# A hybrid decoder layer with 32 experts on one core: expert biases copied into the accumulation banks ahead of each block of tokens, in place of one-hot matmuls

## The reference, cut to what matters

```python
def expert_block(args):
    xe, e = args
    gu = xe @ w_gu[e] + b_gu[e]                 # 1024 -> 2048, gate and up interleaved
    gate = jnp.minimum(gu[..., 0::2], SWIGLU_LIMIT)
    up = jnp.clip(gu[..., 1::2], -SWIGLU_LIMIT, SWIGLU_LIMIT)
    act = (up + 1.0) * (gate * jax.nn.sigmoid(gate * SWIGLU_ALPHA))
    return act @ w_dn[e] + b_dn[e]              # 1024 -> 1024
```

## Time and profile before

| | us |
|---|---|
| median of 3 runs | 1615.03 |
| lowest and highest | 1613.72, 1615.38 |
| profiled execution | 1609.29 |
| its span | 1607.5 |
| PE, DVE, ACT, Pool busy in it | 1479.8, 1293.3, 1020.8, 236.1 |
| granted TensorE clock, mean | 0.956 of full |

### The profile page before, as it was taken

One profiled execution on the slowest core, in us unless ns is written; L12 is line 12 of the kernel. 1 busy time (PEld: TensorE's weight loads), 2 busy tenths in 40 slices (PEclk: granted clock), 3 DMA queues, 4 the chain that ended last, 5 costly groups with the idle time before them and its releaser, 6 DMA issues.

```text
span 1607.5 us, 20866 instructions
## 1 busy us (share of the span) xinstructions
PE 1479.8 (92%) x7011; PEld 1227.5 (76%) x7011; DVE 1293.3 (80%) x1228; ACT 1020.8 (64%) x902; POOL 236.1 (15%) x148
## 2 busy tenths in 40 slices
PE   5999889755899999999999999999999999999983
PEld 5777667644788888888888888888888888888872
DVE  5227753474899999999999999999999999999991
ACT  5335433313677777777777777777777777777771
POOL 0000000000011122211111222111112211111120
PEclk9999999657999999999999999999999999999996
DMA  9311030604899999999999999999999999999974
GB/s 349 105 54 53 27 131 13 223 24 180 304 347 377 385 370 372 382 388 381 388 381 379 375 372 381 385 388 381 387 376 378 375 374 384 385 386 386 377 263 131
DMA packets 97674, 486.12 MB, mean 302 GB/s; under 512 B 8217, under 2 KB 8242, under 8 KB 63794
## 3 DMA queue, kind: packets, MB, share of 16 engines
q1 hardware_dynamic: 87250, 448.05, 71.3%
q0 software_dynamic: 10400, 37.75, 9.0%
HBM read 461.65 MB, written 24.12 MB: 302 GB/s over the span
## 4 chain that ended last, share of the span: by engine, by line
PE 87%; issue 5%; DVE 5%; DMA 2%; ACT 1%; SPq 0%; DVEq 0%; POOLq 0%; POOL 0%; ACTq 0%
PE gu_bank L1031 17%; PE gu_bank L1032 17%; PE gu_bank L1033 17%; PE turn_bank L1031 8%; PE turn_bank L1032 8%; PE turn_bank L1033 8%; PE gu_bank L1226 2%; PE bank L1233 2%; PE bank L1240 2%; PE bank L1031 1%; PE bank L1165 1%; PE bank L1033 1%; PE bank L1032 1%; DVE w_lo L697 1%; PE turn_bank L1148 1%
## 5 line engine op out<-in xcount | busy, mean ns | idle before, releaser
L697 DVE TENSOR_TENSOR w_lo<-raw,w_hi 128x2048 fp32r<-128x2048 f32 x412 | 934.9, 2289 | 129.1 <-ACT w_hi L493 125.0
L493 ACT ACTIVATE w_hi<-raw 128x2048 fp32r<-128x2048 f32 x412 | 789.5, 1920 | 238.9 <-PE gu_bank L1033 184.1
L1031 PE MATMUL gu_bank<-w_hi,turned 128*128 128x512 f32 (+1 forms) x1104 | 432.3, 392 | 7.0 <-DVE turned L950 7.0
L1032 PE MATMUL gu_bank<-w_lo,turned 128*128 128x512 f32 (+1 forms) x1104 | 429.3, 389 | 0.0
L1033 PE MATMUL gu_bank<-w_hi,turned 128*128 128x512 f32 (+1 forms) x1104 | 429.1, 389 | 0.0
L1031 PEld LDWEIGHTS gu_bank<-w_hi,turned 128*128 128x128 f32 x1104 | 208.2, 189 | 49.2 <-issue 5.8
L1033 PEld LDWEIGHTS gu_bank<-w_hi,turned 128*128 128x128 f32 x1104 | 208.1, 188 | 42.8
L1032 PEld LDWEIGHTS gu_bank<-w_lo,turned 128*128 128x128 f32 x1104 | 208.3, 189 | 41.5
L1031 PE MATMUL turn_bank<-w_hi,turned 128*128 128x512 f32 (+1 forms) x544 | 211.5, 389 | 2.0 <-DVE turned L955 2.0
L1032 PE MATMUL turn_bank<-w_lo,turned 128*128 128x512 f32 (+1 forms) x544 | 211.0, 388 | 0.0
L1033 PE MATMUL turn_bank<-w_hi,turned 128*128 128x512 f32 (+1 forms) x544 | 210.3, 387 | 0.0
(11 more groups left out here) (206 smaller groups left out, 1354.5 us busy)
## 6 DMA issues: line engine op xcount, KB each, us to landing
raw<-in_w_gate_up_dram SPq DMA_DIRECT2D x264, 1024.0 KB, 8.8
raw<-in_w_down_dram SPq DMA_DIRECT2D x132, 1024.0 KB, 10.9
raw<-in_w_in_dram SPq DMA_DIRECT2D x10, 1024.0 KB, 8.3
raw<-in_w_out_dram SPq DMA_DIRECT2D x4, 1024.0 KB, 5.2
raw<-in_w_mem_kv_dram SPq DMA_DIRECT2D x2, 1024.0 KB, 8.7
arena<-in_x_dram SPq DMA_DIRECT2D x1, 2048.0 KB, 14.4
arena<-in_position_tables_dram SPq DMA_DIRECT2D x1, 2048.0 KB, 19.5
arena<-in_x_dram SPq DMA_DIRECT2D x2, 1024.0 KB, 5.5
```

Source lines behind the costliest of these rows:

```text
L493: a.activation(w_hi[:, slot, :], raw_ap, ACT.Copy).then_inc(hi_ready, 1)
L697: v.tensor_tensor(w_lo[:, slot, :], raw_ap, w_hi[:, slot, :].bitcast(F32), ALU.subtract).then_inc(lo_ready, 1)
L1031: pe.matmul(bank, a[0], b[0], start=first, stop=False)
L1032: pe.matmul(bank, a[0], b[1], start=False, stop=False)
```

## The change

The split bias tables, `choose`, `gu_bias` and `y_bias` go. For each block SP fetches its two bias rows, 2048 and 1024 values, into one partition (`bias_row`), Pool spreads them over 128 partitions (`spread`), and ACT copies them into the banks: two strided copies of 1024 into `gu_bank` (the second adds 1.0) behind `turn_x`, one of 1024 into `turn_bank` behind `y_out`. All matmuls of a block then accumulate onto that. SP waits with a block's rows for the broadcast of the block before, Pool with the broadcast for the rows and both copies of the last, PE with each sum for the copy. `clamp` waits for the last `gate_up` instead of the bias matmuls. Six matmuls open the banks once.

```diff
@@ SP
+            def biases(e_gu, e_y):
+                sp.dma_start(bias_row[:, 0:2 * FF], b_gate_up[0][e_gu, :]).then_inc(bias_in, 16)
+                sp.dma_start(bias_row[:, 2 * FF:3 * FF], b_down[0][e_y, :]).then_inc(bias_in, 16)
...
             sp.wait_ge(tab_ready, 1)
+            biases(slice(0, 1), slice(0, 1))
             loops = sp.value_load(loops_i[0:1, :], min_val=E - 1, max_val=MAX_LOOPS)
             with sp.Fori(1, loops + 1) as b:
...
+                sp.wait_ge(bias_ready, b)
+                biases(bass.ds(e, 1), bass.ds(before, 1))
                 for k in range(GU):
...
+            sp.wait_ge(bias_ready, loops + 1)
+            biases(bass.ds(e, 1), bass.ds(e, 1))
@@ Pool
-            for i in range(2):
-                pool.dma_start(F[i * E:(i + 1) * E, 0:2 * FF], b_gate_up[0]).then_inc(bias_in_s, 16)
-                pool.dma_start(F[i * E:(i + 1) * E, 2 * FF:3 * FF], b_down[0]).then_inc(bias_in_s, 16)
...
+            def spread(n_in):
+                pool.wait_ge(bias_in, n_in)
+                pool.sem_inc(spread_go, 1)
+                pool.partition_broadcast(bias_rows, bias_row).then_inc(bias_ready, 1)
             gather(slice(0, 1), 1)
+            spread(32)
             pool.wait_ge(xtp_done, 1)
             gather(slice(1, 2), 2)
+            pool.wait_ge(gu_seeded, 1)
+            spread(64)
...
                 gather(bass.ds(b + 1, 1), b * 2 + 1)
+                pool.wait_ge(gu_seeded, b + 1)
+                pool.wait_ge(y_seeded, b)
+                spread(b * 32 + 64)
                 scatter(b - 1, b * 2 + 2)
@@ ACT
+            def seed_gu(n, read=None):
+                a.wait_ge(bias_ready, n)
+                if read is not None:
+                    a.wait_ge(sig_ready, read)
+                banks, rows = (z.rearrange("p (i two) -> p two i", two=2) for z in (gu_psum[:, :], bias_rows[:, 0:2 * FF]))
+                a.activation(banks[:, 0, :], rows[:, 0, :], ACT.Copy)
+                a.activation(banks[:, 1, :], rows[:, 1, :], ACT.Copy, bias=1.0).then_inc(gu_seeded, 1)
+            def seed_y(n, read=None):
+                a.wait_ge(bias_ready, n)
+                if read is not None:
+                    a.wait_ge(y_free, read)
+                a.activation(turn_psum[:, :], bias_rows[:, 2 * FF:3 * FF], ACT.Copy).then_inc(y_seeded, 1)
+            a.wait_ge(banks_open, 1)
+            seed_gu(1)
             turn_x(0, 1)
...
             turn_x(1, 2)
+            seed_gu(2, 1)
             hi_m(GU + 3)
+            seed_y(2)
             with a.Fori(1, loops + 1) as b:
...
                 turn_x(1, b + 2)
+                seed_gu(b + 2, b + 1)
                 for i in range(12, 16):
                     hi_m(GU + i, b)
                 y_out(b * 12 + (16 + GU), bass.ds(b - 1, 1), b * 16)
+                seed_y(b + 2, b + 1)
@@ DVE
-            v.wait_ge(bias_in_s, 64)
-            v.wait_ge(half_used, 16)
-            v.memset(R[2 * E:P, 4 * D:7 * D].bitcast(F32), 0.0)
-            up_bias = bias_in[:, 0:2 * FF].rearrange("p (i two) -> p two i", two=2)[:, 1, :]
-            link(v.tensor_scalar(up_bias, up_bias, 1.0, None, ALU.add))
-            link(v.tensor_copy(bias[0:2 * E, :], bias_in))
-            v.tensor_tensor(bias[E:2 * E, :], bias_in[E:2 * E, :], bias[E:2 * E, :].bitcast(F32),
-                            ALU.subtract).then_inc(bias_ready, 1)
             v.wait_ge(tab_in, 1)
...
-            def clamp(n):
-                v.wait_ge(gu_done, n)
+            def clamp(n, used):
+                v.wait_ge(half_used, used)
...
-                clamp(b + 1)
-                choose(pick, pick_ready, bass.ds(b + 1, 1))
+                clamp(b + 1, b * 12 + (12 + GU))
...
-                v.wait_ge(ybias_done, b)
-                choose(pick_y, pick_y_ready, bass.ds(b, 1))
@@ PE
+            def three_onto(bank, a, b):
+                pe.matmul(bank, a[0], b[0], start=False, stop=False, skip_group_check=True)
+                pe.matmul(bank, a[0], b[1], start=False, stop=False, skip_group_check=True)
+                return pe.matmul(bank, a[1], b[0], start=False, stop=False, skip_group_check=True)
...
-            def gu_bias(n_pick):
-                pe.wait_ge(pick_ready, n_pick)
-                for c in range(4):
-                    ins = pe.matmul(psum[c], pick, bias[:, c * 512:(c + 1) * 512], start=False, stop=True)
-                ins.then_inc(gu_done, 1)
...
+            pe.wait_ge(tab_ready, 1)
+            pe.wait_ge(hi_ready, 17)
+            for c in range(6):
+                ins = pe.matmul(psum[c], act_hi[:, 0, 0:P], w_hi[:, 0, 0:512], start=True, stop=True)
+            ins.then_inc(banks_open, 1)
             turn_rows(16)
+            pe.wait_ge(gu_seeded, 1)
             pe.wait_ge(xlo_ready, 1)
...
             with pe.Fori(1, loops + 1) as b:
-                pe.wait_ge(sig_ready, b)
+                pe.wait_ge(gu_seeded, b + 1)
...
-                gu_bias(b + 1)
                 pe.wait_ge(alo_ready, b * 2)
                 turn_rows(b * 16 + 32)
-                y_bias(b - 1)
+                pe.wait_ge(y_seeded, b)
                 for j in range(DN):
                     down(j, 2 * GU + j, b)
```

More of the change, by code:

```diff
@@ L208, in hymba_layer @@
         idx_scatter = F[:, 15001:15002].bitcast(I32)
-        bias_in = F[0:2 * E, 0:3 * FF]
+        bias_rows = F[:, 0:3 * FF]
+        bias_row = F[0:1, 10752:10752 + 3 * FF]
         h_row = F[:, 4096:5120]
@@ L219, in hymba_layer @@
         ha, la = (R[:, i * D:(i + 1) * D].rearrange("p (k s) -> p k s", k=KT) for i in (2, 3))
-        bias = R[:, 4 * D:7 * D]
-        pick = R[:, 7 * D:7 * D + P]
-        pick_y = R[:, 7 * D + P:7 * D + 2 * P]
         gains_turned, gains_ready = sem("gains_turned"), sem("gains_ready")
@@ L247, in hymba_layer @@
             sem(n) for n in ("chosen_ready", "rank_in", "hot_ready", "tab_in", "tab_ready"))
-        bias_in_s, bias_ready = sem("bias_in_s"), sem("bias_ready")
+        bias_in, spread_go, bias_ready, banks_open, gu_seeded, y_seeded = (
+            sem(n) for n in ("bias_in", "spread_go", "bias_ready", "banks_open", "gu_seeded", "y_seeded"))
         idx_ready, h_in, y_sent, x1_sent = (sem(n) for n in ("idx_ready", "h_in", "y_sent", "x1_sent"))
@@ L251, in hymba_layer @@
         atp_done, ahi_ready, alo_ready = sem("atp_done"), sem("ahi_ready"), sem("alo_ready")
-        pick_ready, pick_y_ready, ybias_done = sem("pick_ready"), sem("pick_y_ready"), sem("ybias_done")
-        gu_done, up_ready, prod_ready, sig_ready, act_ready = (
-            sem(n) for n in ("gu_done", "up_ready", "prod_ready", "sig_ready", "act_ready"))
+        up_ready, prod_ready, sig_ready, act_ready = (
+            sem(n) for n in ("up_ready", "prod_ready", "sig_ready", "act_ready"))
         y_free = sem("y_free")
@@ L956, in turn_act @@
                                 ha[:, 4 * q:4 * q + 4, :].bitcast(F32), ALU.subtract).then_inc(alo_ready, 1)
-            def choose(into, ready, column):
-                v.tensor_scalar(into, cst[:, C_ROWMOD:C_ROWMOD + 1].to_broadcast([P, P]), exp_f[:, column], None,
-                                ALU.is_equal).then_inc(ready, 1)
-            def clamp(n):
-                v.wait_ge(gu_done, n)
+            def clamp(n, used):
+                v.wait_ge(half_used, used)
                 pairs = gu_psum[:, :].rearrange("p (i two) -> p two i", two=2)
@@ L980, in _ @@
             loops = v.value_load(loops_i[0:1, :], min_val=E - 1, max_val=MAX_LOOPS)
-            choose(pick, pick_ready, slice(0, 1))
             turn_x(0, 1)
@@ L988, in _ @@
                 lo_m(i)
-            clamp(1)
-            choose(pick, pick_ready, slice(1, 2))
-            choose(pick_y, pick_y_ready, slice(0, 1))
+            clamp(1, 16 + GU)
             lo_m(GU + 2)
@@ L1217, in gate_up @@
                 for c in range(4):
-                    ins = three(psum[c], (hx[:, k, :], lx[:, k, :]), w_part(slot, c * 512, (c + 1) * 512),
-                                first=k == 0)
+                    ins = three_onto(psum[c], (hx[:, k, :], lx[:, k, :]), w_part(slot, c * 512, (c + 1) * 512))
                 ins.then_inc(half_used, 1)
-            def gu_bias(n_pick):
-                pe.wait_ge(pick_ready, n_pick)
-                for c in range(4):
-                    ins = pe.matmul(psum[c], pick, bias[:, c * 512:(c + 1) * 512], start=False, stop=True)
-                ins.then_inc(gu_done, 1)
             def turn_rows(n_h):
@@ L1242, in turn_acts @@
                 ins.then_inc(atp_done, 1)
-            def y_bias(b):
-                pe.wait_ge(y_free, b + 1)
-                pe.wait_ge(pick_y_ready, b + 1)
-                for c in range(2):
-                    ins = pe.matmul(psum[4 + c][:, :], pick_y, bias[:, 2 * FF + c * 512:2 * FF + (c + 1) * 512],
-                                    start=True, stop=False)
-                ins.then_inc(ybias_done, 1)
             def down(j, i, b):
@@ L1258, in down @@
                         at0 = kk * D + c * 512
```

(8 more changed lines are left out.)

3 lines of the change are left out of this document (removed).

## The result

| | before | changed |
|---|---|---|
| median (20 runs each), us | 1614.24 | 1610.9 |
| lowest and highest | 1609.87, 1616.1 | 1595.16, 1663.54 |
| profiled execution, its span | 1609.29, 1607.5 | 1599.21, 1597.1 |
| ratio to before | | 0.9931, interval 0.9911 to 0.9951 |

The forecast was 1590 us. The change gives 0.7% by the ratio, and 3.3 us by the medians. The changed kernel also scatters: 8 of its 20 executions took over 1615 us, up to 1663.54, which the ratio leaves out, while all 20 of before lie within 6.2 us. The profiled execution is among its short ones.

A forecast was written before the change was run, and what follows sets the result against it. PE was taken to bound the kernel at 35.82 us a pass. Profiled 1609.3 less 5.3 ahead of the loop and 19.8 in it gives 1584.2; the profiled execution being 5.7 under the median, 1590 us was forecast, range 1575 to 1660.

The forecast's parts named there:

- Rivals 2 and 3: Loop: biases late through SP, Pool and ACT, 1655 us, chance 0.14; strided ACT copies at 1.90 us, 1635 us, chance 0.10.
- the rows spread at 14.3: Loop: Pool's broadcast of the bias rows done 14.3 us after half 5's subtraction, 2.3 us to spare.
- rival 1: Loop: a broadcast starting ahead of half 9 or 10 holds DVE 3.1 us; pass 37.9, time 1677 us, chance 0.16.
- the pair's 16.6: Loop: ACT's two copies into the gate and up banks can start 16.6 us after half 5's subtraction.
- the DMA limit of 35.1 us: Loop: share 1.00 against 1.02 when full, so the DMA engines need 35.1 to 35.6 us a pass.
- the forecast pass of 35.2: Loop: the largest of three close limits, PE 34.4, ACT and DVE 34.8, DMA 35.1 to 35.6, taken as 35.2 us.
- the 0.62 that was forecast: Loop: saving per pass, from 35.82 to 35.2 us.
- 11.0 us of landing: Loop: time from SP's issue of a pass's last `down` DMA to its landing, used to place the bias rows.
- 7.9 against a cover of 11.9 us: Loop: the pair is done 7.9 us after the last `gate_up`; PE has 11.9 us of other work, so doesn't wait.
- 5.3 forecast: Ahead of the loop: DVE no longer splits bias tables before the router's table copies, saving 5.3 us.
- a wait that I had costed at nothing: SP: the wait before a pass's 12 DMAs for an earlier broadcast costs nothing, unless the broadcast takes tens of us.
- its 19.8: Loop: total saving, 0.62 us a pass times 32 passes, 19.8 us.

The follow-up runs named there:

- pin_norows: pin_clamp without the two bias row DMAs in the loop, block 0's rows used for all: 1597.58 us, ratio 0.9901.
- pin_clamp: The changed kernel, but Pool's broadcast in the loop also waits until DVE has ended half 10's subtraction: 1593.05 us, ratio 0.9859.
- before_nobias: The kernel before without the loop's six bias matmuls and `choose`, nothing in their place, so no bias is added: 1572.43 us, ratio 0.9729.
- gather_early: pin_clamp with Pool's gather of the next block's rows moved ahead of the scatter: 1588.37 us, ratio 0.9844.
- pool_apart: gather_early, with the scatter also waiting for half 7's subtraction: 1586.85 us, ratio 0.9837.
- pair_behind: pool_apart, with ACT's pair of copies moved behind the rounding of the next block's half 0: 1571.36 us, ratio 0.9735.
- pair_only: pin_clamp with only ACT's pair of copies moved behind the rounding of half 0, Pool's order untouched: 1580.92 us, ratio 0.9808.
- no_pair: pin_clamp without the pair of copies into the gate and up banks in the loop, so results partly wrong: 1581.25 us, ratio 0.9804.
- split_sp: The kernel before; DVE splits bias tables behind the table copies, SP sends block 1's first weights only after the first gather landed: 1601.46 us, ratio 0.9927.

## Why the prediction was wrong

**What held.** PE bounds the kernel before and needs 34.44 us without the six matmuls (34.46 measured). The copies and the broadcast cost what was forecast, and the bias rows' DMAs nothing (`pin_norows`). The broadcast starts where half 10's subtraction ends in 30 passes of the profiled execution. Rivals 2 and 3 didn't occur: no wait of ACT for Pool in the loop, no row of 1.9 us. The forecast contradicts itself in one place that did no harm: it has the rows spread at 14.3, though by rival 1's own argument Pool starts at 12.2 and is done at 15.3, still ahead of the pair's 16.6.

**Rival 1 was no rival but a part of the result, and the largest.** Its mechanism and price were right (37.9 forecast, 37.87 measured, where it stands in every pass), and the landing near half 10 too. The step that failed is the either-or, with a chance of 0.16: the rows were to land 11.2 us after half 5's subtraction and half 10's to run from 10.0 to 12.2, in every pass. In the pass of 38.54 the broadcast began 10.9 us after half 5's subtraction and half 10's 11.0: the subtraction came a us late and the rows 0.3 us early. Of the 0.78 us for which DVE was idle ahead of it, 0.43 stand in before too, though the forecast's order has none; the rest is the wait for the `down` weights. A place that is right by some tenths of a us is missed in part of the passes. With the wait of `pin_clamp` the range is 6 us instead of 68, and the median 1593.05, 3 us from the forecast.
The Trainium skill's rule in SBUF — State Buffer, section Who interferes with whom, that the one that issues first keeps the port until it is done, is borne out in the direction that no row had shown: Pool ahead of DVE, 5.29 us for 2.29.

**The loop: the DMA limit of 35.1 us, read from the share, was none.** `before_nobias` ran below it. That the forecast pass of 35.2 came close to the measured 35.51 is luck. 35.82 less 35.51 is 0.31 us a pass, half of the 0.62 that was forecast. Two steps were missing:
- I asked when the bias rows land, and not when the `down` weights do. I took 11.0 us of landing as given and left the ring through it out: half 4's subtraction, its slot's DMA, half 10's rounding and subtraction, `clamp`. In before, PE kept everything late enough. In the changed kernel ACT waits 49.4 us for it, and the chain goes through that DMA (11.12 us). `gather_early` and `pool_apart` show its part: 35.42 to 35.21.
- I asked whether PE waits for the pair (7.9 against a cover of 11.9 us) and not for what stands behind the pair on ACT. With the prediction's own terms and the rows of the changed kernel, 1.5 from the last `gate_up` to `clamp`, 2.51 + 0.93 + 0.95, the pair 2.05, half 0's rounding 1.96, its subtraction 2.29 make 12.2 against 11.9. The cover does not hold. PE waited 1.00 us in the pass shown (up to 1014.16) and 26.8 us in 31 passes; `pool_apart` keeps 0.45 of it, `pair_behind` a tenth.

The two are coupled, as `pair_only` and `no_pair` show: a pass that PE shortens runs into the landing, and a landing that is shortened leaves PE's gap.

**Ahead of the loop: 5.3 forecast, 8.3 measured, 9.7 counted from the start of the table matmuls.** DVE's wait with the table copies fell from 5.3 us (365.21 less 359.91) to 0.04 (362.17 less 362.13), as forecast. Of this 3.0 us reached the copies, because PE began the table matmuls 1.4 us later in this execution and took 0.8 longer for them (6.47 for 5.66). But the gather then landed in 4.2 us after its issue at 365.99 and not in 9.2. SP now waits with block 1's weights for the first broadcast (371.64), where it sent them beside the gather before (369.29). So 5.0 us came from a wait that I had costed at nothing; 7.6 us remained at the first sum (374.03 against 381.67). `split_sp` shows both without the rest of the change.

**After the loop.** One copy was forecast at up to 1 us. From the last `clamp` to ACT's last `turn_act` it is 15.96 in place of 14.68, and 2.2 to the end of the span.

**By how much.** 25 us were forecast. The profiled execution gained 10.1, the ratio says 11, the medians 3.3. For the profiled execution the loop is 15.5 us short of its 19.8, and the tail 2.2, less 3.0 in favour ahead of the loop. Of the 15.5, 9.4 are the thirty passes of 35.51 in place of 35.2, and 6.1 the first two, in which rival 1 stands. The median is 20.9 us above the forecast, and the wait of `pin_clamp` alone takes 17.9 of them away. That what is left is so small is luck again: passes of 35.42 in place of 35.2 and a longer tail, against more gained ahead of the loop.

## What to carry to other kernels

When work is moved from the engine that sets the pace to another, follow every chain that ends at the pace-setter through the new work, with what stands behind it in the same queue, and check each transfer's own ring, from the freed slot to the next use. In this case a DMA share of 1.00 said that packets were under way, not that the engines were at their rate: compare GB/s in windows, and move small transfers of another queue away from the ones that are waited for. A Pool operation that reads SBUF should be given its place by a wait; left to a DMA's landing, it turns a few tenths of a us into whole subtractions.

## What the runs showed of the hardware

- The exclusion between DVE's subtraction and Pool's broadcast works both ways. Pool ahead of DVE: 5.29 us for a subtraction of 2.29. DVE ahead of Pool: a broadcast recorded with 4.27 where it takes 3.30. Beside `clamp`, which reads at most one operand in SBUF, it took its 3.30 in `pin_clamp`.
- The copies from SBUF into the banks with a step of two take 1.10 to 1.12 us for 1024 columns, the one without 1.03.
- With the scatter and the gather beside them the DMA engines moved 339 GB/s at a share of 1.01, without them 391 at the same share.
- PE began with the gathered 128 rows 4.2 to 5.0 us after the gather's issue with no weights beside it (thirteen profiled executions), and 9.2 us after it with 2 MB issued 0.3 us later (`before` and `before_nobias`).
